# Squares of x through PSUM ahead of two feed-forward networks and stick-breaking, and x's mean one unit of weights later in the memory's values

## What is computed

```
for layer in range(DEPTH):                       # DEPTH = 2
    g = norm_gains[layer]
    hn = rms_norm(x, g[0])
    y = mlstm_mixer(hn, ...) if layer % 2 == 0 else stick_breaking_mixer(hn, ...)
    x = x + rms_norm(y, g[1])
    y = memory_cross_attention(rms_norm(x, g[2]), mem_n, w_q, w_kv, w_o)
    x = x + rms_norm(y, g[3])
    y = swiglu_ffn(rms_norm(x, g[4]), w_gate_up, w_down)
    x = x + rms_norm(y, g[5])

rms_norm(x, gain) = x * rsqrt(mean(x * x, -1) + 1e-6) * gain
```

## Time and profile before

| | us |
|---|---|
| median of 3 executions | 2529.94 |
| lowest and highest | 2526.8, 2530.45 |
| the profiled execution | 2518.72 |
| its span, first to last instruction | 2517.4 |
| PE busy in it | 2402.9 (95%) |
| DVE, ACT, POOL busy in it | 1005.8, 879.3, 1070.3 |

### The profile page before, as it was taken

The page is one execution under the profiler, slowest core; times in us unless marked ns, Lnnn a source line. Parts: engine busy times, 40 slices in busy tenths (PEclk is TensorE's granted clock), DMA queues, the critical chain, the costliest instruction groups (busy, mean ns, idle before and its releaser), DMA issues.

```text
span 2517.4 us, 31056 instructions
## 1 busy us (share of the span) xinstructions
PE 2402.9 (95%) x12860; PEld 2022.4 (80%) x12860; DVE 1005.8 (40%) x1529; ACT 879.3 (35%) x1275; POOL 1070.3 (43%) x811
## 2 busy tenths in 40 slices
PE   7999999999999999999999999998899989999997
PEld 6766877788888787768777888887888988899886
DVE  3236723622211623736236222115573445744403
ACT  4324523422222414745234232224344223422321
POOL 7423733344454441027433444543344433544452
PEclk9999999999999998999999999998999999999999
DMA  4211421222222221013212222222111221222232
GB/s 154 85 58 59 143 84 51 86 99 92 93 101 99 84 92 42 1 59 134 92 51 84 92 100 93 101 93 92 59 35 68 84 76 68 101 93 92 92 103 73
DMA packets 64012, 211.40 MB, mean 84 GB/s; under 512 B 8832, under 2 KB 13056, under 8 KB 63872
## 3 DMA queue, kind: packets, MB, share of 16 engines
q1 hardware_dynamic: 59120, 206.00, 23.4%
q10 hardware_dynamic: 4752, 3.42, 0.5%
HBM read 207.29 MB, written 2.10 MB: 83 GB/s over the span
## 4 chain that ended last, share of the span: by engine, by line
PE 83%; DVE 11%; ACT 3%; issue 2%; DMA 1%; ACTq 0%; POOL 0%; SPq 0%; DVEq 0%
PE ps L404 68%; PE ps L510 5%; DVE u_lo L1457 2%; DVE x L1472 2%; PE ps L735 1%; PE ps L751 1%; PE ps L756 1%; PE ps L802 1%; DVE arena L1470 1%; PE ps L668 1%; PE ps L769 1%; DVE acc L1507 1%; DMA w_land<-in_units 1%; DVE y_ffn L1470 1%; PE ps L426 1%
## 5 line engine op out<-in xcount | busy, mean ns | idle before, releaser
L2096 POOL TENSOR_TENSOR w_lo<-w_land,w_hi 128x512 fp32r<-128x512 f32 x768 | 1025.2, 1360 | 1349.6 <-ACT w_hi L930 1349.4
L404 PE MATMUL ps<-u_hi,w_hi 128*128 128x512 f32 (+3 forms) x2560 | 827.5, 350 | 45.9 <-DVE u_lo L1457 21.7
L404 PE MATMUL ps<-u_lo,w_hi 128*128 128x512 f32 (+3 forms) x2560 | 820.3, 347 | 0.0
L404 PE MATMUL ps<-u_hi,w_lo 128*128 128x512 f32 (+3 forms) x2560 | 816.8, 346 | 0.0
L404 PEld LDWEIGHTS ps<-u_hi,w_hi 128*128 128x128 f32 x2560 | 460.4, 190 | 122.4 <-DVE u_lo L1457 27.5
L930 ACT ACTIVATE w_hi<-w_land 128x1024 fp32r<-128x1024 f32 x384 | 401.3, 1050 | 333.3 <-DMA w_land<-in_units 326.2
L404 PEld LDWEIGHTS ps<-u_lo,w_hi 128*128 128x128 f32 x2560 | 458.1, 190 | 62.8 <-issue 1.7
L404 PEld LDWEIGHTS ps<-u_hi,w_lo 128*128 128x128 f32 x2560 | 458.3, 190 | 60.1
L404 PE MATMUL ps<-hid_hi,w_hi 128*128 128x512 f32 (+1 forms) x594 | 220.2, 371 | 0.0
L404 PE MATMUL ps<-hid_lo,w_hi 128*128 128x512 f32 (+1 forms) x594 | 219.7, 370 | 0.0
L404 PE MATMUL ps<-hid_hi,w_lo 128*128 128x512 f32 (+1 forms) x594 | 219.4, 369 | 0.0
(11 more groups left out here) (304 smaller groups left out, 2831.2 us busy)
## 6 DMA issues: line engine op xcount, KB each, us to landing
w_land<-in_units SPq DMA_DIRECT2D x384, 512.0 KB, 3.2
x<-in_xT SPq DMA_DIRECT2D x4, 528.0 KB, 7.1
arena<-in_memT ACTq DMA_DIRECT2D x2, 1024.0 KB, 5.2
outT<-x SPq DMA_DIRECT2D x16, 128.0 KB, 1.7
arena<-in_masks ACTq DMA_DIRECT2D x1, 448.0 KB, 3.6
arena<-in_consts ACTq DMA_DIRECT2D x1, 296.0 KB, 4.0
consts<-in_consts SPq DMA_DIRECT2D x1, 256.0 KB, 7.8
arena<-in_consts ACTq DMA_DIRECT2D x1, 256.0 KB
```

Of the source, the lines that this page charges most:

```text
L404: ins = pe.matmul(ps[:, bank, at:at + c1 - c0], w, rhs(k, c0, c1)[which], start=first and h == 0, stop=last and h == 2)
L2096: pool.tensor_tensor(w_lo[:, u % LAND, half], w_land[:, u % LAND, half], w_hi[:, u % RING, half].bitcast(F32), ALU.subtract).then_inc(*uni ...
```

## The change

For n = 2, 3 and 5 the two buffers of squares become PSUM banks: 5 and 6 in turn (`SQ_BANK`; even tiles take the bank named, odd tiles the next). ACT writes them there and DVE reads them there. For n = 1 and 4 they stay in banks 6 and 7, for n = 6 and 7 in SBUF. In both cross-attentions x's mean stands behind the fourth unit of the values and no longer behind the third, on PE and, with the two instructions that make `rstd`, on ACT.

```
-        AT_RSTD, AT_ADDEND, AT_SQ = 5, 4, 6
+        AT_RSTD, AT_ADDEND = 5, 4
+
+        SQ_BANK = {1: 6, 4: 6, 2: 5, 3: 5, 5: 5}
...
                     mean(("x", 3 * l + 1), acc, ONE, 6)
-                by_token(f"xa_v{l}", m_tok, 2, [(2, x_mean)])
+                by_token(f"xa_v{l}", m_tok, 2, [(3, x_mean)])
...
                     act.wait_ge(*x_sum.at(summed(n, k - 2)))
-                s_ = acc[:, a:z] if k == 0 else ps[:, AT_SQ + k % 2, 0:z - a] if n in (1, 4) else sq[:, k % 2, a:z]
+                s_ = acc[:, a:z] if k == 0 else ps[:, SQ_BANK[n] + k % 2, 0:z - a] if n in SQ_BANK else sq[:, k % 2, a:z]
                 act.activation(s_, x[:, k, a:z], ACT.Square).then_inc(*x_sq.up())
...
-                    if j == 2:
+                    if j == 3:
                         rsqrt_mean(("x", n), ONE, D, rstd, rstd_at)
...
-                        dve.tensor_tensor(acc[:, c0:c1], acc[:, c0:c1], sq[:, k % 2, c0:c1], ALU.add).then_inc(*x_sum.up())
+                        s_ = ps[:, SQ_BANK[n] + k % 2, 0:c1 - c0] if n in SQ_BANK else sq[:, k % 2, c0:c1]
+                        dve.tensor_tensor(acc[:, c0:c1], acc[:, c0:c1], s_, ALU.add).then_inc(*x_sum.up())
```

More of the change, by code:

```diff
@@ L1702, in x_step @@
                             dve.wait_ge(*x_sum.at(summed(n, k - 1)))
-                        dve.tensor_tensor(acc[:, XS], acc[:, XS], ps[:, AT_SQ + k % 2, 0:S], ALU.add).then_inc(*x_sum.up())
+                        dve.tensor_tensor(acc[:, XS], acc[:, XS], ps[:, SQ_BANK[n] + k % 2, 0:S], ALU.add).then_inc(*x_sum.up())
                 for o in range(DT):
```

## The result

| | before | after |
|---|---|---|
| first comparison: median (executions) | 2528.86 (4) | 2512.97 (4) |
| lowest and highest of these | 2526.8, 2530.45 | 2511.71, 2514.31 |
| the profiled execution | 2518.72 | 2511.71 |
| its span | 2517.4 | 2510.4 |
| all executions of the study: mean (executions) | 2525.5 (99) | 2513.8 (25) |

The account below looks back on a forecast made before the run. PE was taken to bound the kernel, with 83% of the chain. Four terms sum to 10.68 us (7.55 waiting, 3.13 clock); off the median of 2529.94 that gives 2519.3 us, range 2514.5 to 2527.

Parts of the forecast that it names:

- Term 1: Ahead of stick-breaking (n = 3), additions reading squares from PSUM: 2.91 us of PE's wait and 1.58 us of clock, 4.49 us.
- Term 2: Ahead of the feed-forward networks (n = 2 and 5), additions from PSUM: 0.19 us of waiting each, 0.38 us together.
- Term 3: First layer's memory values, x's mean one unit later: 1.47 us of PE's wait gained, no clock.
- Term 4: Second layer's memory values, x's mean one unit later: 2.79 us of waiting and 1.55 us of clock, 4.34 us.
- Rival A: Where PE stood, the clock gives nothing back, falls may come elsewhere; 7.55 us stay, 2522.4 us; chance 0.13.
- B: At n = 3 additions stay slow beside POOL or come too late; 5.81 us stay, 2524.1 us; chance 0.06.
- C: In the values PE waits for POOL's `w_lo`, taking back the moved means' gain; 4.87 us stay, 2525.1 us; chance 0.05.
- D: Slow clock lasts into stick-breaking's 1000 to 1088; slower, 2539.3 us at 20 us of half-clock work; chance 0.03.

Follow-up runs that it names:

- third execution: The kernel before, unchanged, run once more for another profiled execution: 2531.44 us.

## Why the prediction was off, point by point

**Term 1, 4.49 us: right.** The four executions of the changed kernel take 135.16 to 135.21 us in the stage n = 3, the first three of before 139.78 to 139.80: 4.6 us. The seven additions, the absent wait and the clock of 1.00 are as written. The fixed cost of a PSUM source that the Trainium skill gives ("VectorE: DVE Perf Modes", the section on the TRN2 errata) does not show: 687 ns from PSUM against at least 691 from SBUF.

**Term 2, 0.38 us: near in size**, 0.27 and 0.29 us in the kernel with this part alone, and not visible in the time. In the changed kernel nothing of it is left at n = 5: the stage takes 23.54 to 23.63 us there and 23.58 with the means moved and the squares in SBUF. PE comes later by the clock that it lost, and finds the sum ready either way. What the term left out is the neighbour 12 us earlier: the stand of 1.97 us on slow steps beside POOL, worth 3.3 us at each place of the changed kernel, 2.3 of them without the fall behind the stand.

**Term 3, 1.47 us: mis-sized, 3.2 us measured.** The step that failed is "The clock was full here; nothing more." It was full behind the mean; it was not full ahead of it, from 292 to 295 (0.61), and that delay of PE was hidden in the wait. Without the fall the wait is 3.0 us (four executions); with it, 1.3 (three). The fourth unit then fills 2.79 us of waiting instead of 1.47. Whoever reads a wait off one execution has to read the clock ahead of it too: a fall and a wait at the same chain add up to the same moment.

**Term 4, 4.34 us: right.** Values 2 went from a mean of 136.79 in the first three executions of before to 132.40 in the four of after, 4.4 us, with 0.28 us of idle where 0.42 was forecast.

**A term that was missing, -1.0 us at n = 5.** In all five executions with the second mean moved and the stand of 1.97 us left in place, the stage takes 23.54 to 23.63 us; in all others that keep the stand it takes 22.29 to 22.59. This is the part of Rival A that came true: clock given back at one place was lost at another, 150 us on. At n = 2 the same loss comes and goes in before too (22.57, 23.64, 23.65), and was there in all four of after.

**Sum.** 4.6 + 3.2 + 4.4 = 12.2 us at n = 3 and in the values, less 1.0 at n = 5 and 0.4 at n = 2, where the fall comes more often (four of four against two of the first three of before): 10.8 us. Term 2 is no item of its own, since the stages n = 2 and n = 5 hold it. The executions give 11.7; the 0.9 us between the two are in no stage of the table, and both numbers are inside the interval. That the forecast of 10.7 comes so near is in part luck: term 3 was 1.7 us too low, and the losses at n = 2 and 5, which were not in the sum, take 1.4 us and the 0.4 us of term 2.

**The base: the step that put the time outside the range.** "taken off the median the sum gives 2519.3 us". That median was of three executions of a kernel whose executions spread from 2517 to 2533 us, in part by clock falls as the long spell of 8 us. The difference of 11.2 us to the profiled execution was seen and left without a cause. The mean of 99 is 2525.5; from it the sum gives 2514.8, 1.0 us from the 2513.8 of after. Of the 6.3 us between 2519.3 and the 2512.97 of the first comparison, 4.4 are this base, 1.0 is the gain, and 0.8 is that the median of four lies below the mean of all 25 executions of after. Three executions drawn from the 99 have a median of 2529.94 or more about one time in ten, so the high base was bad luck; trusting it to 1.5 us was not. The range allowed that much for it, while its own two numbers, 2518.72 and 2529.94, lay 11 apart; the standard deviation of the 99 is 4.2 us.

**The rivals.** B is refuted by 21 additions of at most 690 ns. C is refuted by the closed-up matmuls behind both means and by values 1 and 2. A holds for 1.4 us of the clock, at n = 5 and 2, not for all. D describes something real, half clock into 1000 to 1012 at 8 us, but the change does not bring it: before has it too, in its third execution.

## What to carry to other kernels

A wait ahead of a matmul and a clock fall ahead of that wait are one quantity; price the removal of a wait by the moment at which the operand is there, not by the idle that one execution lists. Where the profiled execution and the median lie apart by more than the gain, forecast the difference, and give the base a range of its own. VectorE steps with SBUF operands beside GpSimd took 2.3 to 3.3 times their length here (1.61 against 0.70 us, 1.58 against 0.48), and the operand can move or GpSimd can; look also at the steps that feed TensorE, not only at the sums. And where an edit saves 2 us and the time doesn't move, measure the next 100 us too: half clock behind it can take back more.

## What the runs showed of the hardware

- The granted clock after a stand of one length is not one thing: behind 1.96 to 1.97 us it was 1.00 in one stretch and 0.54 in another, reproducibly by kernel at n = 5 (five of five against none of the others). Behind 1.91 us ahead of the first values it was 0.61 in one kernel and 1.00 in the other.
- A fall can last some 13 us or some 40: behind the same stand of 2.74 us the clock came back after some 13 us in one execution and stayed at 0.50 until about 1014 in another, while PE was listed busy for 12.00 of each 12 us.
- POOL is slowed as well: four halves took 6.41 us beside additions with two SBUF operands and 5.06 us beside additions with one.
